# Attention B's value products in two 64-column halves, with the row sums taken by GpSimd and four 32-column products

## The chip, the cores and the metric
The kernel runs on one core of a Trainium2 chip. The metric is the device time of one execution in microseconds, as the median of several runs.

## The reference
One block of a streaming encoder over 1024 positions of width 1024, all float32:

- h = RMSNorm(x), and z = h @ W_in is cut into the inputs of attention A, the inputs of attention B and two gates.
- Attention A is a sliding window with sinks. Attention B has 8 heads and works on compressed queries and keys: q and k have 96 columns per head after their projections (64 plain, 32 rotary, RMS-normed), v has 64. A query sees the keys of its own chunk of 64 positions and of all earlier ones.
- For each head of B: s = q k^T / sqrt(96), p = softmax(s) over the visible keys, y = p v.
- m = sigmoid(gate_A) * (y_A @ W_branch_A) + sigmoid(gate_B) * (y_B @ W_branch_B); x = x + m @ W_out; x = x + relu(RMSNorm(x) @ W_ff1)^2 @ W_ff2.

## The kernel before
All matrices that matter are multiplied as a sum of three products of high and low parts (fp32r), so most of TensorE's time goes to such triples (split_products, L1445). Each engine has one program written out by hand; engines meet at semaphores, and each takes its own instructions in order. The program goes through these stages: norm of x and projection z, the gates with attention A between them, attention B, the branch products (16 of them, L1701), the product with W_out, and the feed-forward part, which is over half of the time.

**Attention B (the loop at L1688).** The work is a list of 96 slots, t = 12 h + r for head h. A slot is one tile of 128 keys against up to 512 queries, transposed: keys lie on the partitions. A head has two query halves. Slots r = 0 to 3 are the four key tiles of the first half, all on the diagonal, with 512, 384, 256 and 128 queries left. Slots 4 to 7 are the four full key tiles of the second half (512 queries each), and 8 to 11 its four diagonal ones (512, 384, 256, 128). In slot t:

- PE makes the scores of t in three passes into one of two PSUM banks (scores_t, L1615). It waits there until ACT has read slot t - 2 (S_RING = 2).
- PE makes the values product of slot t - 2 (values_t, L1633). It is a plain float32 product, which TensorE runs as two matmuls. The stationary operand is v with 64 columns and a 65th column of ones, so that row 64 of the result is the sum of the probabilities. It adds up in PSUM over the slots of the half (bank 5 or 6).
- PE makes one piece of the approximate scores of the next head (approx, L1602), from which DVE takes each query's maximum (row_max, L2064). SP moves the maxima into an extra row of qT (nmax_move, L691), so that the scores come with the maximum taken off.
- PE makes the preparations of the next group of two heads (group_step, L1522). In heads 1 and 3 these are eight projections, in slots r = 0, 1, 3, 4, 6, 7, 9 and 10. In heads 2 and 4 they are eight sets of four transposes in the same slots; the first four sets (r = 0 to 4) need the first half of the tokens, the last four (from r = 6) the second. In head 0 the whole of group 1 is prepared, the second transposes from slot 9.

ACT computes the exponentials of the slot (exp_b, L1312, into p_diag or p_full), reads PSUM for the preparations (group_act) and copies finished halves out (y_out, L1325). DVE reads the preparations as well (group_vec, L1986). Between the projections and the transposes of a group stands GpSimd's chain b_power, b_scale, b_rotate (L947 to L983), once for every four token tiles. Chains 2 and 3 belong to group 1 (head 0); chains 4 and 5 to group 2 (heads 1 and 2); chains 6 and 7 to group 3 (heads 3 and 4). After chain 3 GpSimd splits attention A's result (yA_lanes, L1010), and in head 5 the first weights of the branches (branch_splits, L1027).

**The y chain of a half u.** y_out copies the 65 rows (in odd heads the sum row apart from the rest). SP moves the sums so that they lie on 128 partitions (sum_move, L715), DVE takes reciprocals (L2084), SP stores them to DRAM (L720) and spreads them over 64 rows (L724). DVE multiplies (y_norm, L2095), ACT takes the high part (y_high, L1338), DVE the low part (y_low, L2102). There are two y_raw buffers, so y_out of half u waits for y_low of half u - 2 (the wait on yB_ready):

```
act.wait_ge(slot_done, block_end(u))
if u >= 2:
    act.wait_ge(yB_ready, u - 1)
```

After the last slot the branch products start. The first four need nothing of the last halves, the fifth waits for all of yB_ready (L1717) and for the first gate product on DVE (gate_multiply, L2155), which comes after the last y_low in DVE's program.

## Time and profile before
| | |
|---|---|
| Median of 3 runs | 1390.68 us (1389.57 to 1392.02) |
| The profiled execution: its own time | 1390.65 us |
| Its span, first to last instruction | 1388.8 us |
| Mean granted clock of TensorE | 1.000 |
| PE busy / PE weight loads busy | 1359.0 us / 1112.5 us |
| DVE / ACT / POOL busy | 815.2 / 407.7 / 760.4 us |
| Attention B (first scores to first branch product) | 373.6 to 546.3 us |

Times of the views are microseconds from the start of the span, unless marked ns. PE is TensorE's matmuls, DVE VectorE, ACT ScalarE, POOL GpSimd, SP the engine that issues the DMAs. The end of a matmul in the records is modelled, so what a product costs is read from the start of one to the start of the next. The timeline merges neighbours that are alike (x4 is four of them). A bracket at a row's end is the idle time of the engine before it and what ended it.

### The profile page before, as it was taken

The page shows a single profiled execution, that of the slowest core. Times are in us where ns is not written, and L with a number is a line of the kernel's source. Part 1 is how long each engine was busy: PE and PEld are TensorE (multiplying, and loading weights), DVE is VectorE, ACT ScalarE, POOL GpSimd, SP SyncE. Part 2 cuts the span into 40 slices and gives each one's busy share as a digit, 9 for nine tenths or more (in the row PEclk, how much of TensorE's full clock was granted, in tenths as well). Part 3 has the DMA queues.
Part 4 walks back from the last instruction along what each step waited for, and adds up shares of the span by engine and source line. Part 5 has one row for each costly group of instructions (what it writes and reads, how often), then busy time and mean ns, then how long its engine had stood idle before and what let it go on. Part 6 is the DMA issues. An engine that isn't in the chain of part 4 may idle for free.

```text
span 1388.8 us, 17534 instructions
## 1 busy us (share of the span) xinstructions
PE 1359.0 (98%) x6612; PEld 1112.5 (80%) x6612; DVE 815.2 (59%) x1422; ACT 407.7 (29%) x857; POOL 760.4 (55%) x618
## 2 busy tenths in 40 slices
PE   6999999999999999999999999999999999999998
PEld 6999887668866766888887888888888888888887
DVE  5401725643577773455265667677667777666776
ACT  5113235642355554000033212221221221221121
POOL 2341924445384520354308566668766667866697
PEclk9999999999999999999999999999999999999999
DMA  7120231111111012734101112211111221111113
GB/s 235 44 61 16 86 97 61 65 61 46 41 45 16 10 16 62 247 105 185 43 22 55 53 38 61 62 48 44 54 54 46 61 61 39 54 54 51 48 46 122
DMA packets 102884, 90.82 MB, mean 65 GB/s; under 512 B 21904, under 2 KB 84880, under 8 KB 102800
## 3 DMA queue, kind: packets, MB, share of 16 engines
q1 hardware_dynamic: 102656, 89.17, 21.2%
q8 instruction: 53, 0.87, 0.3%
q10 hardware_dynamic: 144, 0.52, 0.1%
q14 instruction: 31, 0.25, 0.1%
HBM read 76.99 MB, written 12.62 MB: 65 GB/s over the span
## 4 chain that ended last, share of the span: by engine, by line
PE 89%; DVE 3%; POOL 3%; ACT 2%; issue 1%; DMA 1%; ACTq 0%; POOLq 0%; DVEq 0%
PE PS L1451 76%; PE PS L1648 3%; PE PS L1458 2%; PE PS L1823 1%; PE PS L1543 1%; PE PS L1628 1%; PE PS L1612 1%; PE PS L1629 1%; PE PS L1545 1%; PE PS L1630 1%; POOL gw_lo L927 1%; DVE scA L2042 1%; PE PS L1565 1%; DMA r_row<-r_store 0%; PE PS L1580 0%
## 5 line engine op out<-in xcount | busy, mean ns | idle before, releaser
L2226 DVE TENSOR_TENSOR xr<-PS,xr 128x512 f32<-128x512 f32 x240 | 161.7, 684 | 80.5 <-PE PS L1451 80.5
L2226 DVE TENSOR_TENSOR sum<-PS,sum 128x512 f32<-128x512 f32 x168 | 114.0, 686 | 90.8 <-PE PS L1451 90.8
L1451 PE MATMUL PS<-w_hi,u_hi 128*128 128x512 f32 x420 | 163.6, 390 | 0.7 <-DVE u_lo L2230 0.7
L1451 PE MATMUL PS<-w_hi,u_lo 128*128 128x512 f32 x420 | 163.4, 389 | 0.0
L1451 PE MATMUL PS<-w_lo,u_hi 128*128 128x512 f32 x420 | 163.4, 389 | 0.0
L1057 POOL TENSOR_TENSOR w_lo<-w_raw,w_hi 128x512 fp32r<-128x512 f32 x109 | 156.0, 1431 | 9.1
L1451 PE MATMUL PS<-mT_hi,w_hi 128*128 128x512 f32 x512 | 160.4, 389 | 0.0
L1451 PE MATMUL PS<-mT_hi,w_lo 128*128 128x512 f32 x512 | 160.2, 389 | 0.0
L1451 PE MATMUL PS<-mT_lo,w_hi 128*128 128x512 f32 x512 | 160.2, 389 | 0.0
L1386 ACT ACTIVATE relu_t<-PS 128x512 f32<-128x512 f32 x64 | 38.3, 599 | 296.0 <-PE PS L1451 293.0
L869 POOL TENSOR_SCALAR w_hi<-w_raw 128x1024 fp32r<-128x1024 f32 x32 | 39.7, 1241 | 154.7 <-DMA w_raw<-in_w_ff 154.7
L1451 PEld LDWEIGHTS PS<-mT_hi,w_lo 128*128 128x128 f32 x512 | 96.1, 188 | 20.0
L1451 PEld LDWEIGHTS PS<-mT_lo,w_hi 128*128 128x128 f32 x512 | 96.1, 188 | 19.9
L1451 PEld LDWEIGHTS PS<-mT_hi,w_hi 128*128 128x128 f32 x512 | 96.1, 188 | 19.9
L1451 PEld LDWEIGHTS PS<-w_hi,u_hi 128*128 128x128 f32 x420 | 78.8, 188 | 17.9 <-DVE u_lo L2230 1.6
L1394 ACT ACTIVATE u_hi<-u_raw 128x512 fp32r<-128x512 f32 x60 | 36.3, 629 | 192.3 <-DVE u_raw L2237 138.2
L1451 PEld LDWEIGHTS PS<-w_hi,u_lo 128*128 128x128 f32 x420 | 78.8, 188 | 16.4
L1451 PEld LDWEIGHTS PS<-w_lo,u_hi 128*128 128x128 f32 x420 | 78.8, 188 | 16.3
L1060 POOL TENSOR_TENSOR w_raw<-w_raw 128x512 f32<-128x512 f32 x60 | 80.0, 1334 | 19.3 <-PE PS L1451 16.2
L1053 POOL TENSOR_SCALAR w_hi<-w_raw 128x512 fp32r<-128x512 f32 x109 | 88.1, 808 | 0.0
L1451 PE MATMUL PS<-hT_hi,gw_hi 128*128 128x512 f32 x256 | 84.5, 411 | 3.5 <-ACT gate L1212 2.3
L2230 DVE TENSOR_TENSOR u_lo<-u_raw,u_hi 128x512 fp32r<-128x512 f32 x77 | 81.9, 1064 | 0.8 <-ACT u_hi L1389 0.8
(235 smaller groups left out, 2952.8 us busy)
## 6 DMA issues: line engine op xcount, KB each, us to landing
w_raw<-in_w_ff SPq DMA_DIRECT2D x32, 512.0 KB, 4.0
w_raw<-in_w_ff SPq DMA_DIRECT2D x64, 256.0 KB, 2.6
g_raw<-in_w_in SPq DMA_DIRECT2D x16, 512.0 KB, 3.9
gate_store<-gate SPq DMA_DIRECT2D x16, 512.0 KB, 2.6
x_in<-in_x SPq DMA_DIRECT2D x8, 512.0 KB, 10.2
gate_a<-gate_store SPq DMA_DIRECT2D x8, 512.0 KB, 7.8
gate_b<-gate_store SPq DMA_DIRECT2D x8, 512.0 KB, 5.1
raw<-in_w_out SPq DMA_DIRECT2D x8, 512.0 KB, 3.6
```

Source lines behind the costliest of these rows:

```text
L869: pool.tensor_scalar(hi_ap, raw_ap, 1.0, 1.0, ALU.mult, ALU.mult).then_inc(hi_done, 1)
L927: pool.tensor_tensor(gw_lo[0][:, :, :], g_raw[0][:, :, :], gw_hi[0][:, :, :], ALU.subtract).then_inc(gw_ready, 1)
L1053: pool.tensor_scalar(w2_hi[b][:, :], w2_raw[b][:, :], 1.0, 1.0, ALU.mult, ALU.mult).then_inc(w2_step, 1)
L1057: pool.tensor_tensor(w2_lo[b][:, :], w2_raw[b][:, :], w2_hi[b][:, :], ALU.subtract).then_inc(w2_step, 1)
L1060: pool.tensor_tensor(w2_raw[AT[out]][:, :], w2_raw[AT[a]][:, :], w2_raw[AT[b]][:, :], ALU.subtract).then_inc(w2_step, 1)
L1386: act.activation(relu_t[:, :], PS[:, 2 * tile + half, :], ACT.Relu).then_inc(u_act, 1)
L1394: act.activation(u_hi[AT[p]][:, :], u_raw[AT[p]][:, :], ACT.Copy).then_inc(u_act, 1)
L1451: ins = pe.matmul(o, st, cut(mv), start=first and n == 0, stop=last and n == 2)
L1458: ins = pe.transpose(PS[0:rows, bank, i * P:(i + 1) * P], ap, ident[:, :])
L1648: ins = pe.matmul(out[:, c0:HALF], vB[g % 3][:, kt, h % B_GROUP, :], p_tile(t)[:, c0:HALF], start=kt == 0, stop=last)
L2226: dve.tensor_tensor(out, part, out, ALU.add).then_inc(acc_done, 1)
L2230: dve.tensor_tensor(u_lo[AT[p]][:, :], raw_ap, u_hi[AT[p]][:, :], ALU.subtract).then_inc(u_vec, 1)
```

## The change
- v has 64 columns and no column of ones. The values products of four slots are made together (values_group), one group per query half plus one for the full tiles, in slots 4 (j + 1) + 1 for group j; the last one follows after all slots. Two key tiles of a group go to the two 64-row halves of the output bank, so each half of TensorE's columns has its own products. ACT copies one half out (y_out) and DVE adds the other to it (y_add).
- The probabilities are kept in three sets of four tiles (p_set). GpSimd adds them up per head: sums_first makes one tile of the first half's four, sums_full two tiles of the four full ones, sums_last one of the last four, in place. Nine steps of sum_step count them. PE then makes four products of these tiles with 32 columns of ones (sums), one on each quarter of the output partitions, in slot r = 7 of the next head, into one of the two banks that the approximate scores use in turn (USERS, short_bank, wait_short). For the last head the sums are made after the first branch product.
- ACT copies the sums (sums_out), SP moves them in four pieces, DVE adds three of them and takes reciprocals. The y chain of a head runs two heads later: y_norm in slots r = 28 and 29, counted from the head's own slot 0. y_raw has its own place for every head pair, where the low parts then lie.
- On GpSimd the order is new: chains 2 and 3, the adds of head 0, then per head sums_last of the head before, a chain in heads 1 and 3, sums_first and sums_full, another chain. yA_lanes moves from after chain 3 into head 5, the first four branch_splits into heads 6 and 7. The first branch loads move from head 1 to head 5 on SP.

The core of the diff ("..." marks what is left out):

```diff
-P_RING = 3
+SUM_STEPS = 9
+SUM_AT = 7
...
-        vB = [place(f"vB{i}", (195.75, 202, 66.25)[i], [P, T, B_GROUP, V_DIM + 1]) for i in range(3)]
+        vB = [place(f"vB{i}", (195.75, 202, 152.75)[i], [P, T, B_GROUP, V_DIM]) for i in range(3)]
...
+            def sum_move(h):
+                sp.wait_ge(s_read, h + 1)
+                if h:
+                    sp.wait_ge(rsum_b_ready, h)
+                for part in range(4):
+                    sp.dma_start(b_sum[:, part, :], s_raw[32 * part:32 * part + 1, :].rearrange(
+                        "o (p t) -> o p t", t=Q_BLOCK)).then_inc(sum_landed, 16)
...
+                if h == 5:
+                    sp.wait_ge(bT_done, T * B_GROUPS)
                     for e in range(BW_RING):
                         branch_load(e)
                 if more:
...
+            def add_step(h, step, out, a, b):
+
+                pool.wait_ge(sum_step, SUM_STEPS * h + step)
+                pool.tensor_tensor(out, a, b, ALU.add).then_inc(sum_step, 1)
+
+            def sums_first(h):
+                p, d = p_set[0], p_sum[0]
+                pool.wait_ge(p_ready, HEAD_SLOTS * h + Q_BLOCK)
+                if h:
+                    pool.wait_ge(s_done, h)
+                pool.tensor_scalar(d[:, 0:P], p[0][:, 0:P], 1.0, 1.0, ALU.mult, ALU.mult).then_inc(sum_step, 1)
+                pool.tensor_tensor(d[:, P:], p[0][:, P:], p[1][:, P:], ALU.add).then_inc(sum_step, 1)
+                for i in (2, 3):
+                    add_step(h, i, d[:, i * P:], d[:, i * P:], p[i][:, i * P:])
+
+            def sums_full(h):
+                p = p_set[1]
+                pool.wait_ge(p_ready, HEAD_SLOTS * h + 2 * Q_BLOCK)
+                pool.tensor_tensor(p_sum[1][:, :], p[0][:, :], p[1][:, :], ALU.add).then_inc(sum_step, 1)
+                pool.tensor_tensor(p_sum[2][:, :], p[2][:, :], p[3][:, :], ALU.add).then_inc(sum_step, 1)
+
+            def sums_last(h):
+                p = p_set[2]
+                pool.wait_ge(p_ready, HEAD_SLOTS * (h + 1))
+                pool.wait_ge(group_done, 3 * (h + 1))
+                for i in (1, 2, 3):
+                    add_step(h, i + 5, p[0][:, i * P:], p[0][:, i * P:], p[i][:, i * P:])
...
-            for e in range(2 * KD):
+            chain(2)
+            chain(3)
+            sums_first(0)
+            sums_full(0)
+            for h in range(1, B_HEADS):
+                sums_last(h - 1)
+                if h in (1, 3):
+                    chain(4 if h == 1 else 6)
+                if h == 5:
+                    pool.wait_ge(gate_done, 2 * KD)
+                    pool.wait_ge(pv_done, N_A // 2)
+                    pool.wait_ge(y_ready, N_A)
+                    yA_lanes(0)
+                    yA_lanes(1)
+                if h == 7:
+                    branch_splits(2)
+                sums_first(h)
+                sums_full(h)
+                if h in (1, 3):
+                    chain(5 if h == 1 else 7)
+                if h == 5:
+                    yA_lanes(2)
+                    yA_lanes(3)
+                if h == 6:
+                    branch_splits(0)
+                    branch_splits(1)
+                if h == 7:
+                    branch_splits(3)
+            sums_last(B_HEADS - 1)
+            for e in range(4, 2 * KD):
...
-                before = p_tile_before(t)
-                if before >= 0:
-                    act.wait_ge(slot_done, before + 1)
+                j = t // Q_BLOCK
+                if j >= 3 and t % Q_BLOCK == 0:
+                    act.wait_ge(group_done, j - 2)
+                    if j % 3 == 2:
+                        act.wait_ge(s_done, h)
+                    else:
+                        act.wait_ge(sum_step, SUM_STEPS * (h - 1) + (4, 6)[j % 3])
...
+                h, half = u // 2, u % 2
+                act.wait_ge(group_done, 3 * h + 1 + 2 * half)
+                if u == 0:
+                    for b in range(2):
+                        act.wait_ge(gate_stored[b], 16 * KD)
+                act.activation(y_raw[h // 2][head_rows(h), y_cols(half)], PS[other_rows(h), 5 + half, :], ACT.Copy
+                               ).then_inc(y_copied, 1)
+
+            def sums_out(h):
+                act.wait_ge(s_done, h + 1)
+                if h:
+                    act.wait_ge(sum_landed, 64 * h)
+                act.activation(s_raw[:, :], PS[:, short_bank(("sums", h)), :], ACT.Copy).then_inc(s_read, 1)
...
+                for h in range(B_HEADS):
+                    r = t - HEAD_SLOTS * h
+                    if r == 7:
+                        y_out(2 * h)
+                    if r == 15:
+                        y_out(2 * h + 1)
+                    if r == HEAD_SLOTS + SUM_AT + 1:
+                        sums_out(h)
+                    if r in (29, 30):
+                        y_high(2 * h + r - 29)
             y_out(BLOCKS - 1)
+            y_high(BLOCKS - 4)
+            y_high(BLOCKS - 3)
+            sums_out(B_HEADS - 1)
...
+            def values_group(j):
+
+                h, part = j // 3, j % 3
+                half = min(part, 1)
                 u, g = 2 * h + half, h // B_GROUP
-                last = t + 1 == block_end(u)
-                pe.wait_ge(p_ready, t + 1)
-                if kt == 0 and u >= 2:
-                    pe.wait_ge(y_raw_ready, u - 1)
-                if t % (2 * HEAD_SLOTS) == 0 and g < 3:
-                    pe.wait_ge(v_one_ready, g + 1)
-                if t == 0:
+                pe.wait_ge(p_ready, Q_BLOCK * (j + 1))
+                if part < 2 and u >= 2:
+                    pe.wait_ge(y_added, u - 1)
+                if j == 0:
                     pe.wait_ge(gate_ready, 2 * KD)
-                out = PS[0:V_DIM + 1, 5 + u % 2, :]
-                if t == 0:
-                    pe.wait_ge(p_zero_ready, Q_BLOCK)
-                ins = pe.matmul(out[:, c0:HALF], vB[g % 3][:, kt, h % B_GROUP, :], p_tile(t)[:, c0:HALF],
-                                start=kt == 0, stop=last)
-                ins.then_inc(slot_done, 1)
+                if j in (0, 2):
+                    pe.wait_ge(p_zero_ready, Q_BLOCK * (1 + j // 2))
+                for i in range(Q_BLOCK):
+                    own = (i % 2, i in (1, 2))[part != 1]
+                    c0 = P * i if part != 1 else 0
+                    rows = head_rows(h) if own else other_rows(h)
+                    ins = pe.matmul(PS[rows, 5 + half, c0:HALF], vB[g % 3][:, i + Q_BLOCK * (part == 2), h % B_GROUP, :],
+                                    p_set[part][i][:, c0:HALF], start=part < 2 and i < 2, stop=part != 1 and i >= 2)
+                ins.then_inc(group_done, 1)
+
+            def sums(h):
+
+                bank = short_bank(("sums", h))
+                pe.wait_ge(sum_step, SUM_STEPS * (h + 1))
+                if h < B_HEADS - 1:
+                    wait_short(pe, ("sums", h))
+                else:
+                    pe.wait_ge(qk_ready, T * B_GROUPS)
+                if h == 0:
+                    pe.wait_ge(ones_ready, 1)
+                for i, p in enumerate(p_sum + [p_set[2][0]]):
+                    ins = pe.matmul(PS[32 * i:32 * i + 32, bank, :], ones_w[:, :], p[:, :], start=True, stop=True)
+                ins.then_inc(s_done, 1)
...
-                if t >= 2:
-                    values_t(t - 2)
+                if t > Q_BLOCK and t % Q_BLOCK == 1:
+                    values_group(t // Q_BLOCK - 1)
                 a = chunk_at(t)
                 if a is not None:
                     approx(a)
+                if t > HEAD_SLOTS and t % HEAD_SLOTS == SUM_AT:
+                    sums(t // HEAD_SLOTS - 1)
                 for g, p in preparations(t):
                     group_step(g, p)
-            values_t(N_SLOTS - 2)
-            values_t(N_SLOTS - 1)
+            values_group(3 * B_HEADS - 1)
...
+                if e == 0:
+                    sums(B_HEADS - 1)
...
+            def y_add(u):
 
                 h, half = u // 2, u % 2
-                return slice(V_DIM * (h % 2), V_DIM * (h % 2) + V_DIM), slice(half * HALF, (half + 1) * HALF)
+                c = 0 if half else P
+                y = y_raw[h // 2][head_rows(h), y_cols(half, c)]
+                dve.wait_ge(y_copied, u + 1)
+                dve.tensor_tensor(y, PS[head_rows(h), 5 + half, c:HALF], y, ALU.add).then_inc(y_added, 1)
+
+            def sum_reciprocal(h):
+                dve.wait_ge(sum_landed, 64 * (h + 1))
+                if h:
+                    dve.wait_ge(r_stored, 16 * h)
+                link(dve, dve.tensor_reduce(b_rsum[:, 1, :], b_sum[:, 1:4, :].rearrange("p a t -> p t a"), AX.X, ALU.add))
+                dve.reciprocal(b_rsum[:, 0, :], b_sum[:, 0, :])
+                dve.reciprocal(b_rsum[:, 1, :], b_rsum[:, 1, :]).then_inc(rsum_b_ready, 1)
...
+            for part in (0, 2):
+                for i in range(Q_BLOCK):
+                    dve.memset(p_set[part][i][CHUNK:P, i * P:i * P + CHUNK], 0.0).then_inc(p_zero_ready, 1)
...
+                for h in range(B_HEADS):
+                    r = t - HEAD_SLOTS * h
+                    if r == 8:
+                        y_add(2 * h)
+                    if r == 16:
+                        y_add(2 * h + 1)
+                    if r == HEAD_SLOTS + SUM_AT + 3:
+                        sum_reciprocal(h)
+                    if r in (28, 29):
+                        y_norm(2 * h + r - 28)
+                    if r in (30, 31):
+                        y_low(2 * h + r - 30)
+            y_add(BLOCKS - 1)
+            y_norm(BLOCKS - 4)
+            y_norm(BLOCKS - 3)
+            y_low(BLOCKS - 4)
+            y_low(BLOCKS - 3)
+            sum_reciprocal(B_HEADS - 1)
             y_norm(BLOCKS - 2)
-            sum_reciprocal(BLOCKS - 1)
+            y_norm(BLOCKS - 1)
             y_low(BLOCKS - 2)
```

## Rows read from the trace of the kernel before
**Rows 1.** The page, section 4: the chain of waits, shares of the span by engine.
```profile
PE 89%; DVE 3%; POOL 3%; ACT 2%; issue 1%; DMA 1%; ACTq 0%; POOLq 0%; DVEq 0%
```

**Rows 2.** Busy us by stage: length, PE, PEld, DVE, ACT, POOL; clock, DMA share, GB/s.
```profile
373.50:400.20 26.70, 24.60 (x126) 17.94 (x126) 20.09 (x61) 15.39 (x40) 22.92 (x26) 1.00 0.13 33
447.80:473.10 25.30, 25.30 (x122) 19.31 (x122) 18.28 (x63) 14.47 (x42) 9.26 (x11) 1.00 0.11 12
512.30:530.30 18.00, 17.14 (x74) 10.87 (x74) 11.01 (x30) 8.89 (x25) 0.00 (x0) 1.00 0.09 15
```

**Rows 3.** Timeline of POOL: start, duration (us), engine, line, instruction [idle before <- releaser].
```profile
386.13 2.91 POOL L878 TENSOR_TENSOR b_rstd<-b_ms,minus_half 128x16 f32<-128x16 f32 x1 [0.40 <-DVE b_ms L2030]
...
413.18 2.91 POOL L878 TENSOR_TENSOR b_rstd<-b_ms,minus_half 128x16 f32<-128x16 f32 x1 [3.38 <-DVE b_ms L2030]
...
460.75 2.91 POOL L878 TENSOR_TENSOR b_rstd<-b_ms,minus_half 128x16 f32<-128x16 f32 x1 [23.95 <-DVE b_ms L2030]
...
474.42 2.91 POOL L878 TENSOR_TENSOR b_rstd<-b_ms,minus_half 128x16 f32<-128x16 f32 x1 [4.18 <-DVE b_ms L2030]
...
484.39 0.46 POOL L983 TENSOR_TENSOR q_nat<-rtmp 128x128 f32<-128x128 f32 x1
```

**Rows 4.** Timeline of PE, same columns; L1628 opens slots 60, 77 and 80.
```profile
395.76 0.50 PE L1458 MATMUL PS<-ident,q_nat 128*96 128x128 f32 x3 [1.12 <-POOL q_nat L983]
...
438.46 0.60 PE L1458 MATMUL PS<-ident,q_nat 128*96 128x128 f32 x4
...
485.00 0.61 PE L1458 MATMUL PS<-ident,q_nat 128*96 128x128 f32 x4
...
494.44 0.40 PE L1628 MATMUL PS<-qT_hi,kT_hi 97*128 97x512 f32 x1
...
519.68 0.50 PE L1628 MATMUL PS<-qT_hi,kT_hi 97*128 97x512 f32 x1 [0.86 <-ACT p_diag L1321]
...
524.30 0.40 PE L1628 MATMUL PS<-qT_hi,kT_hi 97*128 97x512 f32 x1
...
546.33 0.70 PE L1451 MATMUL PS<-yT_hi,bw_hi 128*128 128x512 f32 x2
```

**Rows 5.** Chain of waits in order of time: start us, length us, what.
```profile
503.78 0.86 PE PS L1648 x2
```

**Rows 6.** Timeline of PE in attention A: L1596 is two 64-column products, four matmuls.
```profile
243.10 0.65 PE L1596 MATMUL PS<-ptA,v_even 128*64 128x256 f32 x4
243.68 0.46 PE L1580 MATMUL PS<-ident,scA 64*128 64x64 f32 x4
...
244.08 0.73 PE L1451 MATMUL PS<-hT_hi,gw_hi 128*128 128x512 f32 x2
244.64 0.62 PE L1451 MATMUL PS<-hT_lo,gw_hi 128*128 128x512 f32 x2
```

**Rows 7.** Groups on POOL in attention B: count | busy us, mean ns | idle before.
```profile
L878 POOL TENSOR_TENSOR b_rstd<-b_ms,minus_half 128x16 f32<-128x16 f32 x6 | 17.5, 2911 | 59.3 <-DVE b_ms L2030 59.3
L1013 POOL TENSOR_TENSOR yT_lo<-yTa,yT_hi 128x1024 fp32r<-128x1024 f32 x4 | 9.8, 2448 | 0.3
```

**Rows 8.** Line 717, moves of sums: issue time on SP (ns), then time to landing.
```profile
L717 SPq DMA_DIRECT2D b_sum<-y_raw x16: 524/594/702, 390.4 to 548.3; - x16
...
DMA to landing us min/median/max: 2.0/2.1/7.0
```

**Rows 9.** Timeline of DVE at the end of the stage.
```profile
555.32 0.18 DVE L2088 RECIPROCAL b_rsum<-b_sum 128x4 f32<-128x4 f32 x1 [3.18 <-DMA b_sum<-y_raw]
...
561.74 0.69 DVE L2098 TENSOR_TENSOR y_raw<-y_raw,r_row 64x512 f32<-64x512 f32 x1 [5.52 <-DMA r_row<-r_store]
...
563.84 1.23 DVE L2160 TENSOR_TENSOR gate_a<-PS,gate_a 128x1024 f32<-128x1024 f32 x1
...
568.42 1.23 DVE L2160 TENSOR_TENSOR gate_a<-PS,gate_a 128x1024 f32<-128x1024 f32 x1 [1.09 <-PE PS L1451]
```

**Rows 10.** Timeline of DVE in head 2.
```profile
431.45 1.44 DVE L2098 TENSOR_TENSOR y_raw<-y_raw,r_row 64x512 f32<-64x512 f32 x1 [0.70 <-DMA r_row<-r_store]
```

199 lines of the change are left out of this document (81 added, 118 removed).

## The prediction, made before the changed kernel was run
> **What bounds the kernel now.** I read the page's chain of waits first: PE carries 89% of it [rows 1]. A busy PE is not a PE at its peak, so the stage that the diff touches has to be read by itself. It is attention B, from 373.6 to 546.3 us, eight heads of 12 slots. The table by stage [rows 2] shows PE nearly full in each head. DVE has 20.1 us of 26.7 in head 0, 18.3 of 25.3 in head 3 and 11.0 of 18.0 in head 6; POOL has 22.9 in head 0 and nothing in head 6. Two things therefore set the pace. In heads 5 to 7 it is PE's own stream. In heads 0 to 4 the GpSimd chain of b_power, b_scale and b_rotate stands between two PE steps: the projections of a group (slots r = 0 to 10 of heads 1 and 3) and its transposes (heads 2 and 4). That chain runs some 9.5 us undisturbed (386.13 to 395.6) and 10.4 at worst (474.42 to 484.85) [rows 3]. PE then waits for it, 1.12 us at 395.76, and at 485.00 it starts 0.15 us after the chain's end [rows 3, 4].
>
> **What the change takes off PE.** A values product of 512 columns takes 0.86 us [rows 5]; by the same rate 384 take 0.65, 256 take 0.43 and 128 take 0.22. A head has six of the first and two of each other: 7.8 us. Afterwards products go to either 64-column half. The trace has this form already, in attention A: two products of 256 columns on the two halves are four matmuls, busy 0.65 us together, and the next instruction starts 0.58 us after the first [rows 6]. In series they would need 2 x 0.43 = 0.86. So halves do run side by side, 0.43 us plus 0.15 behind them; the first pair of gate matmuls afterwards takes 0.73 instead of 0.62 [rows 6], 0.11 more. With some 0.08 on entry, my estimate from the size of these two, a visit to a tiled layout costs 0.34 us. The bounds are 0.15 (the exit alone) and 0.6.
>
> Per head, the two diagonal groups take 1.07 each (640 columns per half), the full group 1.71, and the four 32-column sums 0.86 if all four run together; no row shows four at once, so they cost between 0.86 and 3.4, and I take the first, as the two halves overlap fully. Four visits (three groups, one set of sums) cost 1.36. So 7.8 becomes 3.85 + 0.86 + 1.36 = 6.1: **1.7 us less per head**, 13 us in eight, if PE were alone. The Trainium skill (TensorEngine Tiling (Array Packing), Key Properties) says that a change of tiling mode drains the engine, while it promises up to 2x for 64 columns. The exit of 0.15 us agrees with the first, and it speaks against this change: the visits eat a third of what the halves bring.
>
> **What it puts on the other engines.** GpSimd gets eight additions and a 128-column copy per head. From 1024 columns in 2.45 us and 128 in 0.46 [rows 3, 7], 512 columns are 1.3, 384 some 1.0 and 256 some 0.7. The first group's adds take 2.6 us with their waits, the full group's 2.6, the last group's 2.4: 7.6 us per head, 61 in all. DVE gets two y_add (some 0.65 each) and a reduce per head, and loses one wait on the y chain; ACT loses a copy in odd heads and gains one of 0.6 per head for the sums. SP issues four short moves of sums where it had two, each 0.6 us to issue and 2.1 to land [rows 8]; DVE asks for them three slots later, so they stay hidden. The y chain (copy, norm, high, low) no longer sits between a head's end and the next: PE's idle 0.86 us at 519.68, for an exp that stood behind ACT's wait for y_low, goes [rows 4].
>
> **The sum, from anchor to anchor.** GpSimd runs its queue in order, so its new work is what is late next.
> 1. Up to slot 9 of head 0 the end of chain 3 (395.6 us) decides. It keeps its start, so nothing is gained.
> 2. From there to the start of chain 4 (413.18 [rows 3]) PE loses seven products (4.1 us) and gains one group (1.4). Of these 2.7 I take 2.5, as four transposes must also be drained by ACT and DVE: 410.7. Chain 4 ends at 420.2. Then sums_first and sums_full of head 1 (5.2 us) stand ahead of chain 5 in POOL's queue, where nothing stood: 425.4. Chain 5 adds a gap of 0.4 and 9.7: 435.5. PE came to these transposes at 438.46 [rows 4]. Saved so far: 2.9 us.
> 3. sums_last of head 1 comes behind chain 5 (437.9), and PE wants it for its sums at about 436.8: a wait of 1.1. To the start of chain 6 (460.75 [rows 3]) PE's work falls by 4.1 - 2.05 - 1.2 = 0.85, minus that wait, and by 1.2 in head 3: 456.9. Chain 6, the adds and chain 7 give 466.4, 471.6 and 481.9, against 485.0 [rows 4]: 3.1 saved. DVE has 18.3 of 25.3 us in head 3 [rows 2] and gets 2 more, so I take 3.0.
> 4. In head 4 after that, 0.85 saved is spent on the wait for sums_last. Head 5 started at 494.4 [rows 4] and now starts at 491.4. POOL then has sums_last of head 4, four yA_lanes (3.5 us each, moved here from head 0), two sets of adds and sums_last of head 5: from 494.9 by 2.4 + 13.9 + 5.2 + 2.4 to 518.8. PE wants that in slot 79. Head 5 takes 18.0 - 1.7 - 0.9 = 15.4 (head 6's time before [rows 2], less the change and the y stall), and slots 72 to 79 the 11.9 of before less 4.5 of values and 0.9 of stall, plus 2.8 of groups, 9.3: PE is there at 516.1 and waits 2.7. It leaves for slot 80 at 520.0, where it stood at 524.3 [rows 4]: 4.3 saved.
> 5. From slot 80 to the first branch it took 22.0 us [rows 4]. Values of 11.6 us give way to five groups and one set of sums (9.5), and the last group waits 0.9 for the last exp, where products filled that time. The stalls of about 1.1 us hardly remain: 1.2 more saved, 5.5 at the first branch.
> 6. The sums of head 7 stand behind the first branch: 1.2 back on PE, 4.3 left. Their chain must end before the fifth branch, which starts 21.9 + 1.2 = 23.1 us after the first. The sums end 6.6 us after it, the copy 7.3, four moves 11.2, reciprocals 11.8. From the last reciprocal to the last norm took 6.4 us (555.32 to 561.74), and the gate product came 2.1 later [rows 9]; with two norms instead of one that makes 21.0, and 22.2 with the first gate product. The slack falls from 3 us to 1; I put 0.3 on it.
>
> That makes 4.0 us less. The profiled execution took 1390.65 us, of which 1388.8 is its span, and agrees with the median of 1390.68, so the forecast is **1386.6 us**, 0.3% less.
>
> **A rule that speaks against it.** The y_norm product, two SBUF inputs on DVE, takes 0.69 us at 561.74 with POOL idle and 1.44 at 431.45 with POOL at work [rows 9, 10], and the GpSimd chain itself stretches from 9.5 to 10.4 us. The Trainium skill (SBUF — State Buffer, in its rules on the shared port pair) says why: a VectorE instruction with two SBUF inputs and a GpSimd instruction that reads SBUF shut one another out for the whole instruction. The third rival prices that from the rows.
>
> **Rivals.**
> - *PE alone decides.* The adds slip into gaps, and PE keeps 1.7 us in seven heads and the y stalls of about 1 us in four: some 15 us less, 1375.5. For it: POOL waits 59.3 us for b_ms in this stage [rows 7]. Against: that idle time is not where the chains are. Chance 0.12.
> - *Gain in the last heads only.* DVE, in order and over 70% busy in heads 0 to 4, keeps 373 to 494 us as it is. Steps 4 to 6 give 1.3 + 1.2 - 1.5 = 1.0: 1389.7, no change that can be told. Chance 0.22.
> - *Slower: the adds on GpSimd hold PE.* Place: sums_first, sums_full and sums_last in POOL's queue between the chains of heads 1 to 4 and the lanes of head 5. If the 5.2 us of adds take X more, anchors 2 and 3 move X each, the two waits for sums_last 0.45 X each, and head 5 some 1.9 X: 4.8 X in all. It eats the gain at X = 0.8 and makes the kernel slower by more than 0.2% from X = 1.4, when the adds are 27% slower than those rates. With X = 1.7, a third on top, the time is 1394.8. The chain's own stretch is 10%, DVE's doubling more. Chance 0.19.
> - *The halves do not run together.* Then values stay at 7.8, the sums are 3.4 and the visits 1.4: 4.8 more per head, 1390.7 + 38 less the y stalls, about 1425. [Rows 6] speak against it. Chance 0.03.
>
> **Numbers.** The forecast has 0.44. Its own range is 1383 to 1390, from visits at 0.15 to 0.6 us and X between -0.5 and 0.6. About 0.2% (2.8 us) is what a measurement of this kernel can tell from no change. Faster is most of the forecast (0.41) and the first rival: 0.53. Same is the second rival and the forecast's edge: 0.25. Slower is the last two: 0.22. Leaving out half of the first rival, the last, and the tail of the third gives 1379 to 1394.
>
> **What would show it.** Right: 64-column products that start in pairs and a full group of about 1.7 us; PE idle before the transposes of heads 0, 2 and 4 with GpSimd as releaser, now 2 to 4 us; PE idle at the sums of head 5 for POOL's last add; none in the first four branches. Wrong: PE waiting for nothing but its own stream; halves one after the other; POOL additions of 512 columns far from 1.3 us; the fifth branch late for y_low; or DVE as the releaser of PE's waits.

## The result, and the profile after

The change makes the kernel slower. The median is 1400.71 us in five runs (1396.10 to 1403.46), against 1390.91 of before in the same session: ratio 1.0069, 95% interval 1.0057 to 1.0082. The forecast was 1386.6 with a range of 1379 to 1394, so sign and range were both wrong. The profiled execution of after took 1398.61 us with a span of 1396.8.

Stage by stage, the columns as in [rows 2], heads 0 to 7 of after and then its whole stage:

```profile
373.88:400.73 26.85, 23.14 (x122) 17.60 (x121) 20.51 (x65) 15.78 (x39) 23.14 (x28) 0.94 0.13 33
400.73:424.55 23.82, 23.82 (x131) 17.96 (x129) 16.31 (x58) 13.26 (x38) 13.93 (x19) 1.00 0.09 16
424.55:447.45 22.90, 18.90 (x114) 12.76 (x112) 19.23 (x47) 13.15 (x34) 20.19 (x23) 1.00 0.08 13
447.45:472.07 24.62, 23.79 (x129) 17.84 (x128) 20.56 (x65) 14.37 (x42) 14.66 (x17) 1.00 0.09 12
472.07:495.55 23.48, 21.93 (x114) 14.71 (x112) 19.39 (x47) 13.61 (x34) 20.49 (x24) 0.85 0.09 13
495.55:518.58 23.03, 18.72 (x81) 10.94 (x80) 16.55 (x35) 9.54 (x28) 16.01 (x15) 0.85 0.25 59
518.58:534.97 16.39, 15.47 (x82) 9.86 (x81) 11.97 (x34) 8.98 (x26) 12.35 (x12) 1.00 0.12 18
534.97:552.22 17.25, 14.62 (x78) 8.32 (x76) 6.22 (x13) 8.83 (x26) 14.59 (x17) 1.00 0.10 17
373.88:552.22 178.34, 160.40 (x839) 110.00 (x837) 130.75 (x357) 97.52 (x261) 135.35 (x150) 0.95 0.12 23
```

Heads 1, 2, 4, 5 and 7 of before and its whole stage, in the same columns ([rows 2] has its heads 0, 3 and 6):

```profile
400.20:425.50 25.30, 25.30 (x123) 19.39 (x122) 17.92 (x63) 14.30 (x40) 18.67 (x16) 1.00 0.27 67
425.50:447.80 22.30, 21.01 (x105) 14.05 (x105) 17.94 (x44) 13.31 (x34) 9.69 (x11) 1.00 0.09 13
473.10:494.40 21.30, 20.59 (x105) 14.04 (x104) 17.37 (x44) 13.27 (x34) 10.91 (x13) 1.00 0.10 14
494.40:512.30 17.90, 17.26 (x73) 10.85 (x73) 12.41 (x31) 9.45 (x28) 7.56 (x7) 1.00 0.17 16
530.30:546.30 16.00, 15.38 (x64) 9.22 (x63) 4.67 (x11) 9.11 (x27) 0.00 (x0) 1.00 0.13 19
373.57:546.33 172.76, 166.54 (x782) 115.68 (x781) 119.62 (x340) 98.16 (x263) 79.01 (x82) 1.00 0.14 25
```

The stage took 178.3 us for 172.8. TensorE was busy 160.4 us of it for 166.5, so the work did shrink, but its idle time rose from 6.2 to 17.9 us, and the granted clock, 1.00 throughout before, was at half (1.2 GHz) for 17.1 us: 3.4 us in head 0 and 6.8 each in heads 4 and 5. Heads 1, 3 and 6 are shorter than before (23.8 for 25.3, 24.6 for 25.3, 16.4 for 18.0 us); the other five are longer, head 5 most (23.0 for 17.9). From the first branch (L1533) to the end it is 2.1 us more (844.6 for 842.5).

What the change does on TensorE itself, from its timeline: a set of four sums, a full group and a diagonal group, each with the instruction behind it, the full group also with one ahead and two behind (start us, us, engine, line, operation; a set or group is eight matmuls):

```profile
462.86 0.63 PE L1745 MATMUL PS<-p_sum,ones_w 128*32 128x512 f32 x3 [0.83 <-DVE b_part L2178]
...
463.85 0.59 PE L1625 MATMUL PS<-wuq,cqT 128*128 128x192 f32 x2
...
531.03 0.34 PE L1710 MATMUL PS<-qT_lo,kT_hi 96*128 96x384 f32 x1
531.21 0.34 PE L1711 MATMUL PS<-qT_hi,kT_lo 96*128 96x384 f32 x1
531.48 1.94 PE L1730 MATMUL PS<-p_set,vB 128*64 128x512 f32 x8
533.35 0.44 PE L1693 MATMUL PS<-kT_hi,qT_hi 96*128 96x384 f32 x1
533.62 0.28 PE L1709 MATMUL PS<-qT_hi,kT_hi 97*128 97x256 f32 x1
...
550.99 1.30 PE L1730 MATMUL PS<-p_set,vB 128*64 128x512 f32 x8 [0.46 <-ACT p_set L1392]
552.22 0.50 PE L1533 MATMUL PS<-yT_hi,bw_hi 128*128 128x512 f32 x1
```

From its own start to the next one's, a full group of four 512-column products takes 1.87 us, a diagonal group 1.23, the four 32-column sums 1.00. That is not all of their price: the 384-column products on either side of the full group take 0.27 us each, where the one at 531.03 takes 0.18. Ahead, in and behind, the group costs 0.09 + 0.16 + 0.09, some 0.35 us more than its columns. Head 1, in which TensorE has no idle time in either kernel, shows what all that comes to: 23.8 us for 25.3.

TensorE's pauses, with who ended them:

```profile
396.06 0.80 PE L1540 MATMUL PS<-ident,q_nat 128*96 128x128 f32 x4 [1.99 <-POOL q_nat L1000]
...
438.00 0.61 PE L1540 MATMUL PS<-ident,q_nat 128*96 128x128 f32 x4 [2.03 <-POOL q_nat L1000]
...
440.22 0.63 PE L1745 MATMUL PS<-p_sum,ones_w 128*32 128x512 f32 x3 [0.78 <-POOL p_set L1040]
...
476.49 0.39 PE L1693 MATMUL PS<-kT_hi,qT_hi 96*128 96x256 f32 x1 [1.30 <-DVE b_part L2178]
...
509.59 1.07 PE L1745 MATMUL PS<-p_sum,ones_w 128*32 128x512 f32 x3 [3.15 <-DVE b_part L2178]
...
540.12 0.50 PE L1709 MATMUL PS<-qT_hi,kT_hi 97*128 97x512 f32 x1 [1.71 <-DMA qT_hi<-b_nmax]
...
576.00 0.72 PE L1533 MATMUL PS<-yT_hi,bw_hi 128*128 128x512 f32 x2 [0.48 <-POOL bw_lo L888]
```

What stood behind the pauses that name DVE, and ahead of chain 5, in DVE's timeline:

```profile
426.02 1.16 DVE L2125 TENSOR_TENSOR b_ss<-b_ss,z_ss 128x8 f32<-128x8 f32 x1
427.22 0.17 DVE L2129 TENSOR_SCALAR b_ms<-b_ss 128x16 f32<-128x16 f32 x1
...
473.54 0.47 DVE L2125 TENSOR_TENSOR b_ss<-b_ss,z_ss 128x8 f32<-128x8 f32 x1
474.04 1.20 DVE L2129 TENSOR_SCALAR b_ms<-b_ss 128x16 f32<-128x16 f32 x1
...
502.52 2.32 DVE L2204 TENSOR_TENSOR y_raw<-y_raw,r_row 64x512 f32<-64x512 f32 x1 [0.40 <-DMA r_row<-r_store]
...
506.22 2.50 DVE L2204 TENSOR_TENSOR y_raw<-y_raw,r_row 64x512 f32<-64x512 f32 x1
508.75 0.69 DVE L2178 TENSOR_REDUCE b_part<-PS 128x1 f32<-128x512 f32 x1
```

GpSimd's timeline for the same moments:

```profile
425.88 1.28 POOL L1056 TENSOR_TENSOR p_sum<-p_set,p_set 128x512 f32<-128x512 f32 x1
427.47 2.91 POOL L895 TENSOR_TENSOR b_rstd<-b_ms,minus_half 128x16 f32<-128x16 f32 x1 [0.32 <-DVE b_ms L2129]
...
473.94 1.27 POOL L1056 TENSOR_TENSOR p_sum<-p_set,p_set 128x512 f32<-128x512 f32 x1
475.32 2.91 POOL L895 TENSOR_TENSOR b_rstd<-b_ms,minus_half 128x16 f32<-128x16 f32 x1
...
501.92 2.37 POOL L1030 TENSOR_TENSOR yT_lo<-yTa,yT_hi 128x1024 fp32r<-128x1024 f32 x1
...
505.83 2.34 POOL L1030 TENSOR_TENSOR yT_lo<-yTa,yT_hi 128x1024 fp32r<-128x1024 f32 x1
```

An instruction on 128x8 or 128x16 elements, 0.17 us when alone, takes 1.16 (L2125) and 1.20 us (L2129): each ends 0.02 to 0.03 us after GpSimd's 512-column addition (427.16, 475.21). y_norm (L2204), 0.69 us when alone, takes 2.32 and 2.50 beside the splits of y_A. Each time the row maxima behind it are late. The chains lose less by it: chain 5 starts at 427.47, 0.31 us after GpSimd's own additions, which stood ahead of it anyway, and chain 7 0.11 after them.

### The profile page after: what moved, and what is told of

Same layout as the page of the kernel before. It is cut to its first block, busy times and chain, and to the rows that moved or that the text cites. A ratio compares the mean times of both kernels' runs of the same rounds, so it can differ in the third digit from the quotient of the medians.

```text
span 1396.8 us, 17740 instructions
## 1 busy us (share of the span) xinstructions
PE 1354.8 (97%) x6676; PEld 1107.2 (79%) x6676; DVE 830.6 (59%) x1447; ACT 408.0 (29%) x857; POOL 819.6 (59%) x691
## 3 DMA queue, kind: packets, MB, share of 16 engines
q1 hardware_dynamic: 104832, 89.20, 20.8%
## 4 chain that ended last, share of the span: by engine, by line
PE 85%; DVE 4%; POOL 3%; DMA 3%; issue 2%; ACT 2%; SPq 1%; POOLq 0%; DVEq 0%; ACTq 0%
PE PS L1533 74%; PE PS L1540 2%; PE PS L1924 1%; PE PS L1625 1%; PE PS L1730 1%; DMA r_row<-r_store 1%; PE PS L1693 1%; DMA r_store<-b_rsum 1%; PE PS L1627 1%; POOL gw_lo L944 1%; POOL scA L1007 1%; PE PS L1709 1%; PE PS L1647 1%; DVE scA L2141 1%; PE PS L1710 1%
## 5 line engine op out<-in xcount | busy, mean ns | idle before, releaser
L1533 PE MATMUL PS<-w_hi,u_hi 128*128 128x512 f32 x420 | 163.6, 390 | 0.9 <-DVE u_lo L2346 0.7
L1533 PE MATMUL PS<-w_hi,u_lo 128*128 128x512 f32 x420 | 163.4, 389 | 0.0
L1533 PE MATMUL PS<-w_lo,u_hi 128*128 128x512 f32 x420 | 163.4, 389 | 0.0
L1533 PE MATMUL PS<-mT_hi,w_hi 128*128 128x512 f32 x512 | 160.4, 389 | 0.0
L1533 PE MATMUL PS<-mT_hi,w_lo 128*128 128x512 f32 x512 | 160.3, 389 | 0.0
L1533 PE MATMUL PS<-mT_lo,w_hi 128*128 128x512 f32 x512 | 160.2, 389 | 0.0
L1533 PEld LDWEIGHTS PS<-mT_hi,w_lo 128*128 128x128 f32 x512 | 96.1, 188 | 20.0
L1533 PEld LDWEIGHTS PS<-mT_hi,w_hi 128*128 128x128 f32 x512 | 96.1, 188 | 19.9
L1533 PEld LDWEIGHTS PS<-mT_lo,w_hi 128*128 128x128 f32 x512 | 96.1, 188 | 19.9
L1533 PEld LDWEIGHTS PS<-w_hi,u_hi 128*128 128x128 f32 x420 | 78.8, 188 | 18.0 <-DVE u_lo L2346 1.7
L1533 PEld LDWEIGHTS PS<-w_hi,u_lo 128*128 128x128 f32 x420 | 78.8, 188 | 16.4
L1533 PEld LDWEIGHTS PS<-w_lo,u_hi 128*128 128x128 f32 x420 | 78.8, 188 | 16.3
L1533 PE MATMUL PS<-hT_hi,gw_hi 128*128 128x512 f32 x256 | 84.4, 411 | 3.5 <-ACT gate L1279 2.3
```

The source lines that it names most:

```text
L1533: ins = pe.matmul(o, st, cut(mv), start=first and n == 0, stop=last and n == 2)
```

## The experiments

Theory A: GpSimd's new work holds DVE through the port that they share and its own chains, TensorE pauses, and its clock falls. B: only the splits of y_A, moved to head 5, do it. C: values in groups of four cost by themselves, since they leave ACT and DVE nothing to do and then too much. D, formed later: SP's and DVE's orders. Each run was compared with before on the same chip; "stage" is the time from head 0 to the first branch in the profiled execution, 172.8 in before and 178.3 in after.

### GpSimd's additions

```diff
+w = HALF if h == 0 else 8
-pool.tensor_tensor(p_sum[1][:, :], p[0][:, :], p[1][:, :], ALU.add)
+pool.tensor_tensor(p_sum[1][:, 0:w], p[0][:, 0:w], p[1][:, 0:w], ALU.add)
...
-act.activation(s_raw[:, :], PS[:, short_bank(("sums", h)), :], ACT.Copy)
+act.activation(s_raw[:, :], PS[:, short_bank(("sums", h)), :], ACT.Exp, scale=0.0)
```

> The kernel after with GpSimd's additions of the probabilities cut to 8 columns each in every head but the first (the sums are thus left out, the denominators set to 1 in the copy of the sums; the nine steps, their waits, the four 32-column products and all copies and transfers stay). Theory A (what GpSimd's additions do to the shared port and to its chains, with the clock drops behind the pauses, eats the gain): the DVE instructions L2125 and L2129 are back at 0.17 us, the pause of 1.3 us in head 4 and its clock drop of 6.8 us are gone, the other pauses get shorter; 1389 to 1394 us. Theory B (only the splits of y_A in head 5 cost): nothing of this changes what happens in head 5, so the time stays within 2 us of 1398.6 to 1400.7. Theory C (values in groups of four, and the new waits of TensorE, cost by themselves): also 1397 to 1401.

This kernel leaves out most of the sums. 1393.34 us, ratio 1.0024 (1.0013 to 1.0036); stage 173.3. So additions of full width are worth some 6 us of the 10 (1.0069 less 1.0024), as A has it, and B is out as the whole cause. The pause of 1.3 us in head 4 is gone and the additions no longer hold chain 7; in head 5 a pause of 2.63 us stays, with y_norm at 2.53.

### The clock

```diff
+if hh:
+    filler(bank, {1: 12, 3: 12}.get(g, 0))
 pe.wait_ge(b_normed, 2 * g + hh + 1)
```

> The kernel after with idle products put where TensorE pauses and its clock falls: 12 products of 128 columns ahead of the transposes that wait for the second chain in heads 0 and 4, 8 ahead of the scores product of slot 49, 18 ahead of the sums of head 4; they write a bank that is overwritten or free. They take as long as the pauses or less (0.15 us each from the transposes, 4 in 0.60). If the clock drops behind the pauses cost time of their own (17.1 us at half in the trace of after), the stretches at half speed are gone, and the time falls by 4 to 8 us, to 1391 to 1396. If the pauses alone count and the clock does not, the time is within 1 us of after, or some tenths longer.

1397.89 us, ratio 1.0058 (1.0041 to 1.0074), with a mean clock of 0.998 to 0.999 in its four runs, against 0.993 to 0.996 in after. The stretches at half speed went from 17.1 to 3.4 us, the time fell by 1.5 us by the ratios, and the intervals overlap. The expected 4 to 8 us did not come. That much of the half-speed time lies where TensorE would wait for a chain or a maximum all the same is my reading, and not shown. Within one kernel time and clock go together: after took 1396.10 at 0.996, 1398.61, 1400.71 and 1402.56 at 0.994, 1403.46 at 0.993, though longer pauses would bring both.

One stretch can be priced. g2 (below) has the program of after up to head 4, and its profiled execution had no half-speed stretch in head 0. There chain 4 starts 37.88 us after head 0 does, in after 38.75: the 3.4 us at half cost 0.9 (e1, without one there too, has 37.91). The clock is a part of the loss; how large a part of the whole time stays open.

### The first additions ahead of the chain

```diff
 if h in (1, 3):
+    sums_first(h)
     chain(4 if h == 1 else 6)
-sums_first(h)
+if h not in (1, 3):
+    sums_first(h)
 sums_full(h)
```

> The kernel after with the first four additions of heads 1 and 3 ahead of the chain of that head (a buffer of their own, so they need not wait for the sums products), so that the chain of the next half has no addition beside its statistics. Theory A: L2125 and L2129 take 0.17 us in heads 2 and 4, chain 5 starts 1.2 us earlier (426.3 for 427.47) and ends 436.6, chain 7 1.3 us earlier, the pause at 476.49 shrinks from 1.30 to under 0.4 us and the clock drop behind it (6.8 us at half) goes: 2 to 5 us less, 1394 to 1397. Theory B (only the splits of y_A in head 5) and C (grouping and waits): within 1 us of after. Against A would be the same times with the DVE instructions short.

1399.93 us, ratio 1.0065 (1.0047 to 1.0083): the same time with DVE's instructions short, which is what I had named as speaking against A. The held instructions are cured. The timelines show DVE's two instructions ahead of chain 7, the start of chain 5 on GpSimd, and TensorE at its end. DVE:

```profile
474.77 0.17 DVE L2134 TENSOR_TENSOR b_ss<-b_ss,z_ss 128x8 f32<-128x8 f32 x1
474.98 0.17 DVE L2138 TENSOR_SCALAR b_ms<-b_ss 128x16 f32<-128x16 f32 x1
```

GpSimd:

```profile
426.23 2.91 POOL L900 TENSOR_TENSOR b_rstd<-b_ms,minus_half 128x16 f32<-128x16 f32 x1 [1.91 <-DVE b_ms L2138]
```

TensorE:

```profile
436.74 0.61 PE L1549 MATMUL PS<-ident,q_nat 128*96 128x128 f32 x4 [2.00 <-POOL q_nat L1005]
```

Chain 5 starts 1.24 us earlier, but TensorE still stands 2.00 us before it, and this time the clock fell around the pause (6.8 us at half): head 2 took 24.4 us for 22.9. The pause of 1.30 us in head 4 is gone, but the sums behind it wait 1.66 us for GpSimd's last additions, and the whole profiled execution had 27.3 us at half for 17.1. So curing the held small instructions alone brings nothing that the time shows, and how much of the 6 us of e1 is the port, how much the additions' place in GpSimd's queue, stays open.

### The splits of y_A

```diff
-if h == 5: yA_lanes(0); yA_lanes(1)
 sums_first(h)
 sums_full(h)
-if h == 5: yA_lanes(2); yA_lanes(3)
+if h == 5: yA_lanes(0); yA_lanes(1)
+if h == 6: yA_lanes(2); yA_lanes(3)
```

> The kernel after with the four splits of y_A moved: two behind the additions of head 5, two behind those of head 6 (the branch splits 0 to 3 move into head 7), so that none runs beside the two y_norm of heads 3 and 4 in slots 64 and 65. Theory A and B: y_norm L2204 in head 5 is back from 2.3 and 2.5 us to 0.7, the pause of 3.15 us at 509.6 is under 1 us and the clock drop behind it (6.8 us at half) is gone: 4 to 6 us less, 1393 to 1396. By B alone this brings all of the loss back (1389 or less). If the pause has another cause (the sums' bank, GpSimd's last additions), the time stays within 1 us of after with short y_norm.

1400.40 us, ratio 1.0074 (1.0057 to 1.0091), not the 4 to 6 us less that I expected. y_norm in head 5 is back at 0.69 us, head 5 takes 16.7 us for 23.0 and the first branch starts at 548.22. Then my displaced branch splits cost it again: the last additions stand behind them, and the sums of head 7 wait (TensorE's timeline):

```profile
558.68 1.07 PE L1745 MATMUL PS<-p_sum,ones_w 128*32 128x512 f32 x3 [4.70 <-POOL p_set L1040]
```

> e4_yA_later again, with the second of the three things it moved mended: the branch splits 2 and 3 come behind the last additions of head 7, split 1 just ahead of them, so that the sums of head 7 do not wait for GpSimd (4.70 us in e4). In e4 the first branch began at 548.2 us against 552.2 of after. If the place of the splits of y_A is worth those 4.0 us, the time is 1391 to 1394.5, 4 to 7 us below after. If the gain in head 5 is given back in heads 6 and 7, or in the y tail, 1397 to 1401.

With that mended: 1397.07 us, ratio 1.0059 (1.0037 to 1.0081), and the runs fall in two pairs, 1394.1 and 1394.2, 1399.9 and 1400.2. Stage 173.2, 5.1 less than after, of which the median shows at most 1.4 by the ratios: inconclusive in time, clear in the stage.

> The kernel before with one part of the change alone: the four splits of y_A moved from behind chain 3 (head 0) to head 5. Lock theory: where a split's subtraction runs beside y_norm of head 4, y_norm takes 1.5 to 2.5 us for 0.7, the maxima behind it come late and TensorE waits 1 to 3 us in head 5: 1 to 4 us slower than before. Rival (the splits cost only because the sums product stands in the same banks' queue): the stretched y_norm is there, but TensorE has no pause above 0.6 us in head 5 and the time is before's within 1 us. GpSimd's free time behind chain 3 gains nothing, as chain 4 waits for its own statistics.

The same move put into before alone (the lanes' loop behind a wait for the first exp of head 5): 1391.58 us, ratio 1.0018 (1.0008 to 1.0028). y_norm took 1.94 us and y_low 2.44, and TensorE waited 1.07 us at 500.15 (0.56 in before). So DVE is held without any addition. By the ratio the move costs 1 to 4 us; the profiled execution, the fastest of its ten, shows less: head 5 takes 18.8 us for 17.9, and the stage 173.0 for 172.8.

### The sums' bank

```diff
-return 7 if user == ("sums", B_HEADS - 1) else USERS.index(user) % 2
+return 7 if user[0] == "sums" and user[1] >= 4 else USERS.index(user) % 2
```

> The kernel after with the sums of heads 4 to 6 in a PSUM bank of their own (7, free by then) instead of the two that the row-maximum products use in turn. TensorE's pauses before the sums with DVE's b_part as releaser (3.15, 0.92 us and that of head 6) are then gone. If the wait for the bank is what costs in head 5 (rival of the lock), this brings the 4 us of e4 without moving a split: 1394 to 1397. If the lock on y_norm costs, the pause moves to the next row-maximum product, which waits for the same DVE instruction: 1398 to 1401.

1397.68 us, ratio 1.0062 (1.0045 to 1.0079); stage 173.1. The split stays beside y_norm (2.32 and 2.53 us), and the pause moves to the row-maximum product as the lock theory has it, but is far shorter (TensorE's timeline):

```profile
503.87 0.38 PE L1693 MATMUL PS<-kT_hi,qT_hi 96*128 96x256 f32 x1 [0.59 <-DVE b_part L2180]
...
507.34 0.50 PE L1693 MATMUL PS<-kT_hi,qT_hi 96*128 96x512 f32 x1 [1.19 <-DVE b_part L2180]
```

Head 5 took 18.9 us. The median lies between the range for the bank alone and that for the lock alone, and the trace has both: the 3.15 us were two things in a row: a late maximum, and the sums standing in the queue for its bank.

### Groups of four

```diff
-if t >= 2:
-    values_t(t - 2)
+if t > Q_BLOCK and t % Q_BLOCK == 1:
+    for v in range(t - 5, t - 1):
+        values_t(v)
```

> The kernel before with one part of the change alone: its 65-column values products issued four at a time, one slot behind the fourth exp, in twelve probability tiles as in after (buffers moved as there). No additions, no halves. Theory C (the groups leave the row maxima and exps less time in the slots between, so TensorE waits for DVE, ACT and the transfer of the maxima): 1 to 4 us slower than before, with pauses before the scores of slots 4 of a head. If the groups are neutral (the pauses of after all come from GpSimd and the sums' path), within 1 us of before, or up to 2 us faster, as exps have twelve tiles.

1406.69 us, ratio 1.0131 (1.0114 to 1.0148): some 17 us by the medians, far more than the 1 to 4 expected. The profiled execution, at a clock of 1.000, took 1404.42, 15 above the median of before; the others had 0.996 to 0.999 and took up to 1409.52. It is the largest effect of any single part. GpSimd has no more work in it (78.7 us busy for 79.0). The edit also gives before the twelve probability tiles of after and moves its tiles and first branch loads as there; that these cost nothing is not shown. The whole stage, in the columns of [rows 2]:

```profile
373.80:560.19 186.39, 171.61 (x783) 114.75 (x781) 119.53 (x344) 96.23 (x263) 78.73 (x82) 1.00 0.12 23
```

TensorE in heads 1 and 7:

```profile
411.09 0.47 PE L1607 MATMUL PS<-kT_hi,qT_hi 96*128 96x512 f32 x1 [2.26 <-DVE b_nmax L2072]
...
553.39 0.45 PE L1623 MATMUL PS<-qT_hi,kT_hi 97*128 97x384 f32 x1 [0.86 <-ACT p_set L1318]
...
554.02 3.60 PE L1643 MATMUL PS<-p_set,vB 128*65 128x512 f32 x8
557.06 0.68 PE L1623 MATMUL PS<-qT_hi,kT_hi 97*128 97x256 f32 x1
```

ACT at the same time:

```profile
550.90 0.60 ACT L1318 ACTIVATE p_set<-PS 128x512 f32<-128x512 f32 x1 [2.26 <-PE PS L1625]
...
558.02 0.22 ACT L1315 ACTIVATE p_set<-PS 64x64 f32<-64x64 f32 x1 [3.26 <-PE PS L1625]
```

While the burst at 554.02 runs (3.04 us to the next product) ACT has nothing to do (3.26 us idle), as only two score banks exist and both are used up; afterwards a score product waits for an exp (0.86 us at 553.39, behind two copies of y). ACT is only a part of it. TensorE's longer waits in the stage add up to 5.8 us for DVE's row maxima (2.26 of them at 411.09), 5.2 for exps and 1.3 for the transfer of the maxima, where before had 1.4, 2.5 and none. All its idle time rises from 6.2 to 14.8 us. The other 5.1 us of the longer stage are busy time (171.6 for 166.5) with the same products, which I can't account for.

> The kernel after with the values products issued two key tiles at a time, in every second slot, in place of four in every fourth; the diagonal pairs are then 512 with 384 and 256 with 128 columns, not balanced. TensorE has more to do: 0.43 us more for the columns of the two diagonal groups and three more visits of some 0.15 to 0.3, 0.9 to 1.3 us per head or 7 to 10 us in all. Theory C (bursts leave ACT idle, and the score products between them then wait for exps and row maxima): the time rises by less than 4 us or falls, since pauses on ACT and on the transfer of the maxima in heads 5 to 7 go. If bursts do not matter, all of it shows: 1407 to 1411.

The reverse in after, products in pairs:

```diff
-if t > Q_BLOCK and t % Q_BLOCK == 1:
-    values_group(t // Q_BLOCK - 1)
+if t >= 3 and t % 2 == 1:
+    values_pair((t - 3) // 2)
```

1400.22 us, ratio 1.0069 (1.0052 to 1.0085), the same as after. A pair takes 1.00 us (512 with 512, 512 with 384) or 0.57 to the next start, and there are three more visits, each with its edges of 0.09 us ahead and behind. Head 1, without a pause, took 25.3 us for the 23.8 of after: 1.5 us more work per head, some 12 in eight (an estimate), and nothing of it shows in the time. In after the bursts of four cost about what their lighter work brings.

### What is left without the additions, and the best orders

> f1 with GpSimd's additions cut to 8 columns as in e1 (the sums left out, the denominators 1). This shows what the change takes off TensorE when GpSimd neither adds nor splits y_A beside y_norm. Theory A: the gain of e1 (first branch at 546.3 for 552.2) and that of e4 (548.2 for 552.2) add, the first branch begins at 541 to 543, and the time is 1386 to 1389: faster than before, near what was forecast. If grouping, visits or the copies cost more than forecast, the first branch stays at 544 or later and the time above 1389.5.

e1 and f1 together: 1390.61 us, ratio 1.0008 (0.9999 to 1.0018), level with before. The stage, in the columns of [rows 2]:

```profile
373.80:543.97 170.17, 157.27 (x839) 108.68 (x837) 124.32 (x357) 97.60 (x261) 93.38 (x147) 0.97 0.12 24
```

The first branch begins at 543.97, later than the 541 to 543 expected. TensorE is 9.3 us less busy than before even with 10.2 us at half clock, but 12.9 us idle, of which 2.00 at 396.00 and 2.01 at 437.14 wait for GpSimd's chains and 1.61 at 531.10 for the transfer of the maxima. Stage 2.6 us shorter, the rest 1.3 longer. So even a GpSimd without additions does not give the forecast gain.

> f1 with the early first additions of heads 1 and 3 (e3) and 12 idle products ahead of the transposes that wait for the second chain in heads 0 and 2 (e2). With the lock theory the two gains add up, since they sit in different heads: 1.3 us at the chain of head 2, 1.3 at that of head 4 and no clock drop behind the pauses of 2.0 us: 2 to 4 us below f1, 1388 to 1391. If GpSimd's queue as a whole is the bound (the last additions of head 3 behind chain 7 hold the sums by 1.7 us in e3 and e4 alike), the moves gain nothing behind that wait and the time is f1's within 1 us.

1395.00 us for the 1388 to 1391 expected, ratio 1.0036 (1.0023 to 1.0048), stage 172.1, clock 0.996 to 0.998: below f1 by more than its own spread, though the two intervals overlap.

> The same as h2 with the values in groups of four. The gains of e3, f1 and g2 sit in different heads (1.3 at the chain of head 2; the splits; the bank): 1389 to 1393, against 1397.1 of f1 and 1397.7 of g2. If the splits and the bank are two cures for the same pause, it is within 1 us of the better of them, 1396 to 1398.

1393.72 us, ratio 1.0028 (1.0018 to 1.0037), stage 170.9.

> The early additions (e3), the moved splits (f1), the sums of heads 4 to 6 in their own bank (g2), and the values in pairs (h1). By theories A and C together the pauses for DVE, GpSimd and ACT in heads 4 to 7 are under 4 us in all and the first branch starts before 546.3: 1387 to 1392. If pairs only cost TensorE, it is 3 to 8 us above the next kernel.

1392.99 us, ratio 1.0024 (1.0014 to 1.0033), stage 170.5. The two are the same in time: early additions, moved splits and the own bank together take 4 to 5 parts in a thousand off after, and shorter bursts give back the 1.5 us of work per head that they cost. Their stages are 2 us shorter than that of before, but from the first branch to the end they take 845.9 and 847.5 us for its 842.5. In h2 no pause over 1.4 us was left behind head 0, but neither beats before.

> f3 (narrow additions, moved splits, 1390.6 us) with the bank of g2 and the values in pairs. It shows what TensorE, ACT and DVE alone allow with short bursts. Theory C: the pauses of f3 in head 7 (1.61 us on the transfer) and the clock drop behind it go: 1386 to 1389. If the work of the pairs outweighs it, 1391 to 1396.

1391.55 us, ratio 1.0013 (1.0003 to 1.0023), stage 169.5, not the 1386 to 1389 expected: against h2 narrow additions bring 1.4 us, with intervals that overlap, once the splits and the bank are right. Other orders thus seem to bring most of the 6 us of e1, though these kernels differ from e1 in more than that.

### SP's and DVE's orders

```diff
-if r == HEAD_SLOTS + SUM_AT + 3:
+if r == HEAD_SLOTS + SUM_AT + 4:
     sum_reciprocal(h)
...
-nmax_move(h + 1, 6); reciprocal_store(h - 1); nmax_move(h + 1, 7); reciprocal_spread(h - 1)
+nmax_move(h + 1, 6, 7); reciprocal_store(h - 1); reciprocal_spread(h - 1)
```

> The kernel after with two orders changed, no work: DVE takes the reciprocals of the sums behind the last maximum of the head (slot 23 for 22) and SP sends the last row maxima ahead of the reciprocals; the branch weights 4 to 7 are loaded ahead of the last reciprocals. Theory D (DVE's and SP's order behind the four sums moves holds the row maxima of the next head, and the branch weights): the pause before slot 88 (1.71 us on the transfer of the maxima) shrinks to under 0.7, the pause of 0.48 for the fifth branch's weights goes, the time falls by 1.5 to 3 us, 1397 to 1399 against 1400.4 of after. If only GpSimd matters (theory A), the pauses go, and GpSimd's last additions or the exp take their place: within 1 us of after.

1409.39 us, ratio 1.0141 (1.0124 to 1.0158), 10 us worse than after: a clear miss. The pause before slot 88 fell from 1.71 to 0.87 us, but the spread of the reciprocals came too late for y_norm, which waited on DVE ahead of the row maxima (1.92 us at 527.76), and head 6 took 20.4 us for 16.4. The larger part lies behind the stage: with four branch loads ahead of the last reciprocals the fifth branch waited 4.79 us for the gate product, and the rest took 850.3 us for 844.6. In DVE's order, y_norm's slot leaves the reciprocals no slack at all.

> f2 (1395.0 us) with the orders of g1 and the bank of g2. If these pauses are the remainder (in f2 0.56 and 1.46 us on the transfer of the maxima, 0.49 and 1.37 on the bank, 2.17 on the branch weights), 1389 to 1392, level with before. Under 1388 would mean that the clock is regained too; above 1394 that each pause only hides the next wait, for an exp or for GpSimd.

1401.57 us, ratio 1.0075 (1.0049 to 1.0100). It contains g1's orders, and shows them again: head 6 took 21.0 us, and the fifth branch waited 5.27 us for the gate product.

> h2 (1393.0 us) with the branch weights 4 and 5 loaded ahead of the last reciprocals on SP, so that the fifth branch does not wait for GpSimd's split of them (1.36 us in h2). The gate product is ready 1.0 us before the fifth branch starts in h2, so this can bring 1.0 us at most: 1391.5 to 1392.5, if SP's order is what holds that branch. If the y chain of head 7 holds it, nothing: 1393.

1395.18 us, ratio 1.0032 (1.0022 to 1.0042). The first branch began at 542.87, 3.5 us before that of before, and all of it went in one wait of TensorE, for the gate product ahead of the fifth branch:

```profile
569.86 1.19 PE L1542 MATMUL PS<-yT_hi,bw_hi 128*128 128x512 f32 x2 [3.36 <-DVE gate_a L2289]
```

The two loads put ahead of the reciprocals delayed their spread (issued at 562.27 for 561.20 in h2, although the stage ended 1.4 us earlier); behind the pause the clock stood at half for 6.8 us. So SP's order was not what held the fifth branch: the y chain of head 7 was right behind it.

> i1 with the two diagonal groups of a head issued four at a time again (balanced, two visits less) and only the full group in pairs. If the long burst of the full group (2 us) is what leaves ACT idle, this has the lighter work of h3 and the short bursts of h2: 1389 to 1391.5, level with before. If any burst of four costs, it is i1's time or more.

1398.04 us, ratio 1.0059 (1.0046 to 1.0073), worse than i1: TensorE waits 2.26 us for the transfer of the maxima in head 7, and 3.42 for the gate product. Its stage had 10.2 us at half clock where that of i1 had none, so whether the bursts or the clock did it stays open.

## Why the prediction was wrong, step by step

- **What the change takes off PE**: right, in kind and in size. Halves and the four sums run side by side. A visit costs 0.35 us with its two edges, for 0.34, so a head's products come to the forecast 6.1 us. Head 1 had 1.5 us less (23.8 for 25.3), for 1.7. GpSimd's additions took what [rows 3, 7] gave: 1.27 for 512 columns, 1.00 for 384.
- **Step 1** held in the start of the transposes (396.06), but the pause before them grew from 1.12 to 1.99 us, and the clock was at half for 3.4 us behind it, which cost 0.9 us. The sum had no term for the clock, since [rows 2] show 1.00 everywhere.
- **Step 2 failed**, and first at its first anchor. Chain 4 was to start at 410.7, 2.5 us earlier than before; it started at 412.63, 0.55 earlier. Of the 1.9 missing, 0.3 are step 1's later transposes and 0.9 the clock; 0.7 stay open. The additions then took 5.1 us (5.2 forecast) and ended at 427.16, chain 5 started at 427.47 for 425.8 and ran 10.35 us for 9.7, to 437.8 for 435.5. 2.9 us were to be saved, 0.5 were (438.00 for 438.46). The wait for sums_last (0.78 us for 1.1) held.
- **Step 3 failed.** Chain 6 started at 459.27, not 456.9, and ran 10.9 us for 9.5; chain 7 ended at 484.8 to 485.2, not 481.9. With the pause of 1.30 us behind the held L2129 and 6.8 us at half clock, head 5 began at 495.55, where 491.4 was forecast and before had 494.44.
- **Step 4 failed.** I had GpSimd's last additions as the releaser (2.7 us in slot 79). Instead the splits of y_A held y_norm, y_norm the maximum, and the maximum the sums' bank: 3.15 us, in slot 67, with DVE as the releaser, which the forecast had named as a sign of its being wrong; in slot 79 the wait was 0.92, for DVE too. I had the rule on the port in the text, with 1.44 us for y_norm from [rows 10], and priced it only as slower additions. DVE can be the one that is held, and a long GpSimd instruction holds a short one for its whole rest. The Trainium skill (SBUF — State Buffer, Who interferes with whom) says both: a VectorE instruction with two SBUF inputs waits out a GpSimd one that reads SBUF, and so does a tensor_scalar in a two-port mode. The trace agrees for the first kind (L2125 at 1.16 us and y_norm at 2.32 have two SBUF inputs); L2129 (1.20 us), a tensor_scalar, was held as well, but no run shows which mode it was in.
- **Step 5 failed.** From slot 80 (529.82) to the first branch it took 22.4 us, where 20.8 was forecast and before had 22.0. 1.71 us of it are a wait for the transfer of the maxima before slot 88, and 0.47 and 0.46 waits for exps. "The last group waits 0.9 for the last exp, where products filled that time" is what groups do at every boundary. Single products between the score products were the cover under which ACT made the next exps and DVE the next maxima. I costed the regrouping at its columns and visits and put the loss of this cover at nothing everywhere else; in g4 that part, with the tiles and loads moved as it needs, costs before some 17 us.
- **Step 6** was too small: 2.1 us more after the first branch, not 1.2. The sums of head 7 took the forecast 1.2 with their edges, and the fifth branch waited 0.48 for weights whose load stands on SP behind the reciprocals (issued 11.7 us after the first branch in before, 17.0 in after), a queue that I had not walked through.

The third rival, adds on GpSimd that hold PE, was the side on which it ended, though not by its mechanism: the additions were not 27% slower. It also stopped at 1394.8.

Shown: additions some 6 us (e1), the grouping some 17 us in before (g4), the splits beside y_norm 1 to 4 us in before (f4), stretched instructions and their cure (e3, f1), 0.9 us for one stretch at half clock (g2). Open: how much the clock costs in all (e2: 1.5 us, intervals overlapping); how the 6 us of the additions divide between GpSimd's queue and the port; and how much of after's loss the grouping is, since pairs bring more work with them (h1). The parts overlap and don't add up to the 10 us. Not tried: more than two score banks with groups of four, and sums of head 7 ahead of the first branch, which would shorten the y chain.

## What to carry to other kernels

Before products are gathered into bursts, look at what the other engines do in the gaps that vanish: here two score banks and single values products kept ACT and DVE ahead of TensorE, and a burst of 3 us left ACT idle for 3.26. When work goes to GpSimd, list DVE's small instructions beside it, since each can be held for the rest of GpSimd's instruction, and all that DVE has behind them with it. A saving on the busiest engine ends at the next chain that does not shrink: here GpSimd's 10 us chain in heads 0, 2 and 4, and the way from the last sums to the first gate product.

## What the runs showed of the hardware

- Four 32-column products of 512 columns, on four column groups, take 1.00 us together to the next start (after, 462.86 to 463.85), where one 65-column product takes 0.86. With what the products ahead and behind lose, a visit to halves or quarters costs some 0.35 us over its columns (after, 531.21 to 533.62).
- TensorE's granted clock fell to half for 3.4 or 6.8 us (once 10.2, in e3) near the end of some pauses or up to 2 us behind them, and not at others of the same length: behind 1.99 us at 396.06 in after, not at 2.03 at 438.00; in f1 at both. With idle products at the three places where it fell in after (e2) it stayed at 1.00 there, and fell once elsewhere.
- GpSimd's own instructions stretch too: one on 128 columns took 0.92 us for 0.46 at 434.71 in after, beside y_norm on DVE (434.42 to 435.30).
